# Seams and down steps of a one-core decoder layer: norm, gate and up ahead of their blocks, weight sums by accumulating transfers

## The reference

```
h = rmsnorm(x, norm1_g);  z = h @ w_in            (q, k, v, gates of two attention kinds)
compressed keys/values:  gelu(rows @ cmp_w1 + b1) @ cmp_w2   over cached rows, by a page table
x = x + concat(rmsnorm(o_fox), rmsnorm(o_nsa)) @ w_out
gu = rmsnorm(x, norm2_g) @ w_gu;  g, u = halves of 2816 columns
gc = conv_b + sum_i conv_w[i] * g_ext[i : i+T]     (3 taps; the last two rows of g are outputs too)
y = x + (silu(gc) * u) @ w_down;   output rmsnorm(y, final_norm_g)
```

## Time and profile before

| | us |
|---|---|
| median of 3 runs | 2007.82 (2004.02 to 2010.42) |
| profiled execution, its own time | 2004.98 |
| its span | 2003.1 |
| TensorE busy | 1814.0 (91%) |
| VectorE / ScalarE / GpSimd busy | 997.1 / 730.9 / 532.3 |
| mean granted TensorE clock | 0.969 of full |

### The profile page before, as it was taken

The page is one execution under the profiler, slowest core; times in us unless marked ns, Lnnn a source line. Parts: engine busy times, 40 slices in busy tenths (PEclk is TensorE's granted clock), DMA queues, the critical chain, the costliest instruction groups (busy, mean ns, idle before and its releaser), DMA issues. The chain is left out here.

```text
span 2003.1 us, 31175 instructions
## 1 busy us (share of the span) xinstructions
PE 1814.0 (91%) x11465; PEld 1594.2 (80%) x11465; DVE 997.1 (50%) x1890; ACT 730.9 (36%) x1457; POOL 532.3 (27%) x624
## 2 busy tenths in 40 slices
PE   4997999998876799999997998999999999799995
PEld 4897777998644588888886887999999999776684
DVE  3233421333333678787777543223333233456997
ACT  3233411211321277777777332111211112132352
POOL 5020022421453342222212102111222111243552
PEclk9798999999998899999998998999999999899998
DMA  7533353346987992233312221111111111254443
GB/s 184 82 98 137 111 164 123 112 159 212 313 243 263 174 237 66 64 69 69 82 46 77 74 83 44 53 42 42 42 52 50 44 42 52 82 183 161 177 143 127
DMA packets 169719, 229.25 MB, mean 114 GB/s; under 512 B 44928, under 2 KB 113369, under 8 KB 169467
## 3 DMA queue, kind: packets, MB, share of 16 engines
q1 hardware_dynamic: 143118, 152.77, 25.9%
q0 software_dynamic: 24400, 72.81, 13.1%
q10 hardware_dynamic: 2080, 2.10, 0.3%
HBM read 192.65 MB, written 40.24 MB: 116 GB/s over the span
## 5 line engine op out<-in xcount | busy, mean ns | idle before, releaser
L121 PE MATMUL gate_acc<-o_T_hi,w_gate_split_hi 128*128 128x352 f32 x528 | 171.6, 325 | 2.3 <-ACTq L2749 2.3
L121 PE MATMUL up_acc<-o_T_hi,w_up_split_hi 128*128 128x352 f32 x528 | 170.4, 323 | 0.7 <-DVEq L2792 0.7
L122 PE MATMUL gate_acc<-o_T_lo,w_gate_split_hi 128*128 128x352 f32 x528 | 170.4, 323 | 0.0
L123 PE MATMUL gate_acc<-o_T_hi,w_gate_split_lo 128*128 128x352 f32 x528 | 170.2, 322 | 0.0
L122 PE MATMUL up_acc<-o_T_lo,w_up_split_hi 128*128 128x352 f32 x528 | 169.2, 321 | 0.0
L123 PE MATMUL up_acc<-o_T_hi,w_up_split_lo 128*128 128x352 f32 x528 | 169.2, 320 | 0.0
L2285 ACT ACTIVATE pa_scores<-pa_scores,pa_neg_max 128x128 f32<-128x128 f32 (+1 forms) x192 | 143.4, 747 | 15.6 <-DVE pa_neg_max L2325 12.4
L121 PE MATMUL y_acc<-w_down_split_hi,act_split_hi 128*128 128x512 f32 x308 | 124.8, 405 | 19.6 <-DVE act_split_lo L3110 19.0
L2835 POOL TENSOR_TENSOR w_gate_split_lo<-w_gate,w_gate_split_hi 128x1024 fp32r<-128x1024 f32 x21 | 50.4, 2401 | 341.7 <-ACT w_gate_split_hi L2759 341.7
L2373 DVE TENSOR_TENSOR pa_probs_T_lo<-pa_t,pa_probs_T_hi 128x512 fp32r<-128x512 f32 (+2 forms) x240 | 123.9, 533 | 28.6 <-ACT pa_probs_T_hi L2300 26.1
L2300 ACT ACTIVATE pa_probs_T_hi<-pa_t 128x512 fp32r<-128x512 f32 (+2 forms) x240 | 110.9, 477 | 66.6 <-PE pa_t L2224 63.6
(11 more groups left out here) (447 smaller groups left out, 4758.2 us busy)
## 6 DMA issues: line engine op xcount, KB each, us to landing
w_down_raw<-in_w_down SPq DMA_DIRECT2D x59, 512.0 KB, 4.3
fox_k_pages<-in_cache_fox_kv SPq DMA_DIRECT2D x64, 256.0 KB, 6.4
w_rows<-in_cache_fox_kv POOLq DMA_DIRECT2D x48, 256.0 KB, 8.5
w_gate<-in_w_gu SPq DMA_DIRECT2D x22, 512.0 KB, 3.9
w_up<-in_w_gu SPq DMA_DIRECT2D x22, 512.0 KB, 4.0
w_rows<-in_w_in SPq DMA_DIRECT2D x5, 2048.0 KB, 9.5
sel_pages<-in_cache_nsa_kv POOLq DMA_DIRECT2D x64, 128.0 KB, 8.4
pa_k_fox<-scratch_kf_d POOLq DMA_DIRECT2D x32, 256.0 KB, 6.7
```

Of the source, the lines that this page charges most:

```text
L121: pe.matmul(out, a[0][at], b[0][bt], start=start, stop=False)
L122: pe.matmul(out, a[0][at], b[1][bt], start=False, stop=False)
L123: return pe.matmul(out, a[1][at], b[0][bt], start=False, stop=stop)
```

## The change

It makes these edits, as one (in `project` VectorE's order changes as ScalarE's does):
- `front`: ScalarE's first weight loads wait for the page table. The turns come at j % 4 == 1 in place of j % 5 == 3. SyncE loads the gain and tiles 2 and 3 when ten products are done; ScalarE squares and takes roots of tiles 0 and 1 after the tenth gelu, VectorE scales them. `project` starts with `turn_x(0)`. Some buffers lie elsewhere.
- `gate_up`: the last two column blocks are written out. The edge transposes lie between the last up products, ScalarE copies them, SyncE stores them piece by piece. The last multiplication goes in thirds. GpSimd makes the first two act sums of `down`, ScalarE and VectorE split its step 0. Their buffers are placed by a class `DownAhead`.
- `down`: starts with step 0 split. Weight sums of products 3, 4 and 6 (those with a plus) are made by a transfer that GpSimd issues with an add onto the landed load; GpSimd's own sums remain for products 1 and 2. All act sums are VectorE's. The adds, squares and scalings are spread; of the last four tiles, the right halves are squared and multiplied by the gain under product 6, the last product's tiles are added one by one, and ScalarE scales the right halves beside VectorE.

```diff
 def front(c):
-                    if j % 5 == 3 and between:
+                    if j % 4 == 1 and between:
                         turn(between.pop(0))
...
+            act.wait_ge(s_pt, 48)
             load_w1(act, 0)
             load_w1(act, 1)
...
+            sp.wait_ge(s_hid, FIRST_DONE)
+            sp.dma_start(c.n1_g[:, :], d["norm1_g"][0:1, :].to_broadcast([P, D])).then_inc(c.s_n1g, 16)
+            for t in range(2, 4):
+                sp.dma_start(c.n1_x[t][:, :], d["x_prompt"][0, t * P:(t + 1) * P, :]).then_inc(c.s_x1[t], 16)
...
                 gelu(m)
+                if m + 1 == FIRST_DONE:
+                    for t in range(2):
+                        norm.squares(act, t)
+                    for t in range(2):
+                        norm.root(act, t)
...
+            for t in range(2):
+                norm.mean(dve, t)
+            for t in range(2):
+                norm.scale(dve, t)
             results(NBAT - 1)
 def project(c):
-            squares(0)
-            root(0)
             rounded(0, [0])
-            squares(1)
-            root(1)
-            rounded(0, [1])
             copy(0)
-            rounded(0, [2, 3])
+            rounded(0, [1, 2, 3])
             copy(1)
 def gate_up(c, hT, act_T, gate, ahead):
+            for n in range(3):
+                for k in range(KD):
+                    ins = split_products(pe, U_[:, n, 0:CH], ws[1], hT, np.s_[:, k, :],
+                                         np.s_[:, k, n * CH:(n + 1) * CH], k == 0, k == KD - 1)
+                    if k == KD - 1:
+                        ins.then_inc(s_ul, 1)
+                    if n == 0 and k in (3, KD - 1):
+                        turn_edges(2 * (k // 4))
+                        turn_edges(2 * (k // 4) + 1)
+                    if n == 1 and k == 3:
+                        turn_edges(4)
+                        turn_edges(5)
...
+            silu(LAST, 1)
+            act.wait_ge(ahead.s_first, 16)
+            act.activation(ahead.ws0[0][:, :], ahead.first[:, 0, :], ACT.Copy).then_inc(s_ph, 1)
+            act.wait_ge(s_pa, 1)
+            act.activation(ahead.a_s0[0][:, :], ahead.a_sum[0][:, :], ACT.Copy).then_inc(s_ph, 1)
...
+            pool.wait_ge(s_g, NF + 1)
+            for k in range(2):
+                pool.tensor_tensor(ahead.a_sum[k][:, :], act_T[:, k, HT:T], act_T[:, HF + k, HT:T], ALU.add).then_inc(s_pa, 1)
 def down(c, act_T, ahead):
-    W_POOL = [len(b) > 1 for a, b, o in PRODUCTS]
-    A_POOL = [len(a) > 1 and len(b) == 1 for a, b, o in PRODUCTS]
-    A_DVE = [len(a) > 1 and len(b) > 1 for a, b, o in PRODUCTS]
+    W_DMA = [len(b) > 1 and b[1][1] > 0 for a, b, o in PRODUCTS]
+    W_POOL = [len(b) > 1 and b[1][1] < 0 for a, b, o in PRODUCTS]
+    A_DVE = [len(a) > 1 for a, b, o in PRODUCTS]
...
+        ADD_AT = {p: (1, 2, 3, 4) if p == 5 else (1, 3, 5, 7) for p in range(1, NPD)}
+        SQUARES_AT = {2: 8, 3: 4, 4: 5, 5: 6, 6: 7}
+        SCALED_AT = [(5, 10), (6, 0), (6, 2), (6, 4), (6, 6)]
+        GAINED_AT = [(6, 6), (6, 8), (6, 9), (6, 10)]
...
-                    for i, ((fh, ch), sign) in enumerate(PRODUCTS[p][1]):
+                    for i, ((fh, ch), sign) in enumerate(PRODUCTS[p][1][0:1] if W_DMA[p] else PRODUCTS[p][1]):
...
+                if p == 6 and k in (3, 5, 7, 9):
+                    t = T1_TILES[k // 2 - 1]
+                    act.wait_ge(s_v, 5 * NPAIR + t + 1)
+                    square(t, 4, HW, D)
             for i, t in enumerate(T1_TILES):
                 act.wait_ge(s_v, 6 * NPAIR + i + 1)
-                square(t)
+                square(t, 0, 0, HW)
...
+            for i, t in enumerate(T1_TILES):
+                act.wait_ge(s_yg, i + 1)
+                act.activation(y[:, t, HW:D], y[:, t, HW:D], ACT.Copy, scale=ss[:, 3, t:t + 1]).then_inc(s_yr, 1)
...
+                if W_DMA[p] and k % 2 == 0:
+                    n = chunk_of[k]
+                    k0, m = CHUNKS[n]
+                    b, count = loaded_at[p, n]
+                    (fh, ch), sign = PRODUCTS[p][1][1]
+                    pool.wait_ge(s_r[b], count)
+                    pool.dma_start(raw[b][:, 0, 0:m, :], w_d[:, fh * HF + k0:fh * HF + k0 + m, ch * HW:(ch + 1) * HW],
+                                   accum_op=ALU.add).then_inc(s_ra[b], 16)
```

More of the change, by code:

```diff
@@ L169, in front @@
         ohc = flat[1][:, :].rearrange("p (m n) -> p m n", m=16)
-        xt = [split(ph, f"cmp_rows_T{k}", [P, SB, G, 8, CP]) for k in range(2)]
+        xt = [tuple(xt_first), split(ph, "cmp_rows_T1", [P, SB, G, 8, CP])]
+        norm = FirstNorm(c)
+        FIRST_DONE = len(steps) - 2
         hs = ph.sb("cmp_hidden", [P, 4, SB * G * 64])
@@ L687, in project @@
         lp = [ntp[0][:, 0:4, :], ntp[0][:, 4:8, :], ntp[1][:, 0:4, :]]
-        s_g = ph.sem("n1_gain_loaded")
-        s_ss, s_ms, s_rt, s_rr, s_xn = (ph.sem(f"n1_{n}") for n in ("squares", "mean", "root", "inverse", "normed"))
+        s_xn = norm.s_xn
         s_nt, s_nh, s_nl = (ph.sem(f"n1_{n}") for n in ("turned", "copied", "rest_kept"))
@@ L882, in _ @@
                 if ci == 0 and t + 2 < NR:
-                    squares(t + 2)
-                    root(t + 2)
+                    norm.squares(act, t + 2)
+                    norm.root(act, t + 2)
                 if ci and t == 1 and ci + 1 < len(chunks):
@@ L910, in scale @@
             def scale(t):
[L911 to L920, removed]
-                dve.scalar_tensor_tensor(out=xn[t % 2][0:rows, :], in0=x[t % 4][0:rows, :], scalar=rr[0:rows, t:t + 1],
-                                         in1=g[0:rows, :], op0=ALU.mult, op1=ALU.mult).then_inc(s_xn, 1)
+                norm.mean(dve, t)
+                dve.wait_ge(s_nt, t - 1)
+                norm.scale(dve, t)
             def rest(t):
@@ L2773, in _ @@
             columns(1, 1)
-            with act.Fori(1, NF // 2) as i:
+            with act.Fori(1, NF // 2 - 1) as i:
                 for b in range(2):
@@ new lines, in _ @@
+                    multiplied(2 * i + b, b)
+            chain.leave(NF // 2 - 1)
+            chain.enter(0, 2 * 3)
+            convolved(LAST - 1, 0)
+            multiplied(LAST - 1, 0)
+            convolved(LAST, 1)
+            for n in range(3):
+                dve.wait_ge(s_ul, n + 1)
+                dve.tensor_tensor(act_T[:, LAST, n * CH:(n + 1) * CH], gc[1][:, n * CH:(n + 1) * CH], U_[:, n, 0:CH], ALU.mult)
+                if n == 1:
+                    dve.wait_ge(s_ph, 1)
+                    dve.tensor_tensor(ahead.ws0[1][:, :], ahead.first[:, 0, :], ahead.ws0[0][:, :], ALU.subtract)
+                    dve.wait_ge(s_ph, 2)
+                    dve.tensor_tensor(ahead.a_s0[1][:, :], ahead.a_sum[0][:, :], ahead.a_s0[0][:, :], ALU.subtract)
@@ L2847, with down @@
 ]
-def down(c, act_T, first, s_first):
+def down(c, act_T, ahead):
     nc, d = c.nc, c.d
@@ L2880, in down @@
         s_r = [ph.sem(f"w_down_loaded{i}") for i in range(RB)]
+        s_ra = [ph.sem(f"w_down_summed{i}") for i in range(RB)]
         s_x = ph.sem("x1_loaded")
@@ L2910, in down @@
                 b = (p * NCH + n) % RB
-                loads[b] += 16 * len(PRODUCTS[p][1])
+                loads[b] += 16 if W_DMA[p] else 16 * len(PRODUCTS[p][1])
                 loaded_at[p, n] = (b, loads[b])
+                if W_DMA[p]:
+                    summed[b] += 16
+                    summed_at[p, n] = (b, summed[b])
         def sums_before(s):
-            return sum(W_POOL[p] or A_POOL[p] for p, k in steps[:s])
+            return sum(W_POOL[p] for p, k in steps[:s])
         def w_raw(p, k, i):
@@ L3269, in build @@
                 c.s_kq = [keep.sem(f"q_nsa_split_stored{i}") for i in range(2)]
+                c.n1_stats = [keep.sb(f"n1_{n}", [P, len(ROWS)]) for n in ("ss", "ms", "rt", "rr")]
+                c.s_n1g = keep.sem("n1_gain_loaded")
+                c.s_n1 = [keep.sem(f"n1_{n}") for n in ("squares", "mean", "root", "inverse", "normed")]
                 far_end(c)
```

336 lines of the change are left out of this document (206 added, 130 removed).

## The result

The changed kernel takes 1979.44 us in the median of 4 runs (1977.63 to 1982.66), the kernel before 2007.19 (2004.02 to 2010.42) beside it: ratio 0.9863, 95% interval 0.9842 to 0.9885. The forecast was 1967.7 with 1957 to 1984. So 27.8 us were won where 40 were reckoned.

| stage, by TensorE's starts | before | after | won | forecast |
|---|---|---|---|---|
| start to last matmul of the compression | 178.93 | 174.01 | 4.9 | 6.3 |
| from there to product 1 of the projection | 23.60 | 16.12 | 7.5 | 7.4 |
| from there to the first gate matmul (unchanged code but for the tail of `project`) | 1016.21 | 1016.87 | -0.7 | 0 |
| gate and up, to the first matmul of down | 524.32 | 515.74 | 8.6 | 8.7 |
| down, to its last matmul | 243.57 | 240.50 | 3.1 | 13.7 |

What follows compares the result with a forecast made beforehand. TensorE, busy 91%, was taken as the bound, with its idle stretches to win and VectorE pacing products 3, 4 and 6 of down. Ten terms summed to 40.1 us, giving a median of 1967.7 us, range 1957 to 1984.

Steps and rivals of the forecast that it cites:

- tail: After the last matmul: first store at +3.6 us and not +7.6; 4.0 us won, bounds 3 and 5.5.
- first norm: Into the projection: squares, roots and scaling hidden under earlier products, product 1 sooner; 7.4 us, bounds 6.0 and 8.5.
- gate/up into down: Hand-over to down: edge transposes moved between up products, stores landing first; 8.7 us won, bounds 7.5 and 9.4.
- Clock in product 0: Start of down: TensorE's shorter stop keeps the granted clock up in product 0; 1.7 us won, below is 0.
- Products 2 and 3: Down: 1.2 and 0.9 us won; T, from GpSimd's seeing the load to the sum's landing, taken at 5.7 us.
- Steady state: Down: with three buffers turning and chunks of 5.49 us, an accumulating transfer of up to 9.5 us is hidden.
- Products 4 and 6: Down, without GpSimd's weight sums: 32.96 to 30.3 us (2.7 won) and 38.05 to 30.8 (7.2 won).
- Rival 3: Down: VectorE still the bound in products 3, 4 and 6, act sums staying at 1181 ns; 1978.5 us, chance 0.06.
- Start: Kernel start: ScalarE's loads wait for the page table, so rows start near 7.6 us, not 10.10; 2.5 won, bounds 0 and 3.3.
- Turns: Compression: transposes at j = 1, 5, 9 remove three stops of 1.27 us; 3.8 us won, bounds 1.5 and 3.8.
- Rival 2: The seams give half: clock low, start bound by later weights, last-sequence rows late; 24.1 becomes 12, 1980 us, chance 0.12.
- rival 1: Down: slow accumulation at 12.2 us, stalls of 24.8 us where 2.05 was forecast; 1990 us, chance 0.12.

Runs made afterwards that it cites:

- the two kernels with the filler: Six unused 352-column matmuls before down, on half buffers with product 3's first two chunks, then all its sums, by GpSimd: 1974.15 and 1971.62 us.
- the chunks on time: Changed kernel, but from product 3 on a chunk takes half a buffer, so six chunks are in flight, not three: 1971.25 us (0.9824).

## Why the prediction was right, and where its sum was off

The direction and the range held, by the hand-overs and the tail: **first norm** 7.5 for 7.4, **gate/up into down** 8.6 for 8.7, **tail** 3.7 for 4.0. Down, the core of the argument, did not come so: 3.1 for 13.7. The forecast's first sign of being wrong did appear, TensorE waiting in products 3, 4 and 6 for ScalarE's rounding behind a transfer; the second, a gain under 21 us, did not. And the range held partly by luck. The spreading of the adds was worth 6.9 where 1.2 was reckoned; without these 5.7 the time would have been near 1985 by my estimate (1979.4 + 5.7), outside the range. The terms:

- **Clock in product 0**, 1.7: 0.1. "TensorE stood 9.34 before it; now it stands 2.4" took it that the shorter stop would do. It stood 2.36, and the granted clock is 0.95 as it was 0.94. After a stop of 1.80, in the two kernels with the filler, it stayed up.
- **Products 2 and 3**, +1.2 and +0.9: they lost 1.0 and 1.4. T was taken at 5.7 and measured 6.6 in the median, with loads of 4.7 and not 3.5; but at this seam it was 6.0 and 6.5, and the second chunk of product 3, the one that I had priced, stopped TensorE for 1.26 where 2.05 was reckoned. The graver slip is which chunk was priced. The first stands behind the sample rows in the same way, and stopped TensorE 1.45 at the end of product 2 and 0.79 in product 3 through VectorE's late add. The chunk at the end of product 3 stopped it for another 1.29.
- **Steady state**, "T up to 9.5 is hidden": the 5.49 of a two-step chunk was used throughout, but each product ends in a chunk of one step. Across the seam into product 4 a buffer was free at 1851.95 and its chunk due, split, at 1866.63: 14.7, not 16.5. A load of 5.3, 0.3 to GpSimd's issue, an accumulation of 8.4 and 2.0 of splitting make 16.0: 1.3 late.
- **Products 4 and 6**, 2.7 and 7.2: 1.6 and 3.8. With the chunks on time they are 30.2 and 30.45, 0.1 and 0.35 better than forecast. In the changed kernel product 6's steps from k = 1 to 4 take 3.0 us and not 2.74, VectorE's own work in them (three instructions of 0.6 and an add or scaling of 1.2): the forecast's two steps of lead, which were to cover this, are not there. That a late chunk had taken them is argued; with the chunks on time these steps take 2.74.
- **Their reason**, "There VectorE is the bound, and its act sum takes 1181 ns ... stretched while GpSimd adds weights", took three products as one. The 1181 is the median over all three; in product 3 it was 1660, in product 6 677. In product 3 the cause was wrong: with eight of eleven act sums still stretched TensorE doesn't stop once the adds are spread, so it was the six adds in one step that had stopped it. In product 6 GpSimd's sums did hold VectorE up, but through the scalings, 2.31 for 1.27: it takes 36.0 and 36.3 with the adds spread and the sums on GpSimd, and 30.45 without the sums once the chunks are on time.
- **The accumulating transfers**, credited with what products 3, 4 and 6 were to win, cost some 2 us in down in the form the change gives them: in the first execution 1.6 in product 2 and 3.5 in product 3 against 2.1 won in product 6. With product 3 left to GpSimd and half buffers behind it they win 6.6, of which 5.8 in product 6. Rival 3 (act sums that stay at 1181 for another reason) did not come: in the changed kernel none takes over 694 ns.
- **Start**, 2.5: at the first matmul 1.0 in the profiled execution, 0.4 on average, and none of it by the wait; the lower bound was 0. The first rows are issued 4.3 us sooner, more than reckoned, but the weights now go out beside them. The cover "TensorE would wait for rows anyway" was the right thing to ask about and was not priced.
- **Turns**, 3.8: the stops went, the rows of the last sequences came late, the reason given for the lower bound of 1.5; 0 to 2.6 by execution, so some lie below that bound.

Rival 2 (seams half) is what the front did; rival 1's mechanism is what down did, at T = 6.6 instead of 12.2. The estimate of T by the Trainium skill, 4.4 where T measured 6.6, rested on two rules: 3.2 us for 512 KB on GpSimd's queue (DMA: Bandwidth & Descriptors, Anatomy of one DMA), where this stage's plain transfers take 4.6, and the measurement decides; and a reduction that costs by its second source read (Collectives: The Full Stack, The bandwidth ceiling), where the add cost 2.0 of 6.6. The second agrees in kind with the doubled engine share; whether read or add takes it, no run here tells apart.

## What to carry to other kernels

Before an operation is moved to another engine or to the queues, spread the lumps on the engine that seems bound: in product 3 an engine busy 99% of the time held nobody up once its adds were spread. Then look at each product and each instruction by itself: a median over three products hid that in one of them the adds cost and in another the scalings. A transfer that waits for a transfer needs its lead counted at the shortest chunks and at every seam where buffers are held, first chunk included, with the duration it has among others in flight. And two loads into a buffer that become one load and an addition leave half the buffer free: use it for that lead.

## What was not expected of the hardware

- An accumulating transfer of GpSimd's queue went in twice the packets of a plain one (4478 for 2400 over the same 8.6 MB) and held the DMA engines nearly twice as long (38.4% for 20.8%); 6.6 us for 4.6 at 512 KB. With several of them in flight some took 14 and 15 us to land.
- TensorE's granted clock was at its lower level for part of the first step after a stop of 2.36 us in nine of ten executions (0.62 in the mean of that step in the first), and at full level after one of 1.80, with six more matmuls ahead of it, in both.
- GpSimd's sums stretch some of VectorE's act sums from 0.68 to 1.67 us and its scalings from 1.27 to 2.31. In product 3 the first cost TensorE nothing once the adds were spread; in product 6 the second went with 36.3 us for 30.45.
